# Sums of squares, inverse roots and weight preparation of a hybrid convolution and attention block, moved and rewritten

## What is computed

```python
xn = rms_norm(x, norm_mix_g)
z = xn @ w_in                      # columns B | C | h | q | k | v, 512 each
y_conv = B * (conv3(C * h) + b)    # causal, three taps per channel
q, k = rms_norm(q, q_gain), rms_norm(k, k_gain)       # over each head of 64
s = q @ k_band.T / 8 + bias        # 64-position chunks, band of 9 chunks
o = softmax(s) @ v_band
y = concat(group_rms_norm(y_conv), group_rms_norm(o)) # groups of 64
x = x + y @ w_out
xn = rms_norm(x, norm_mlp_g)
x = x + square(relu(xn @ w1)) @ w2                    # 4096 hidden
# rms_norm(v, g) = v * rsqrt(mean(v * v) + 1e-6) * g
```

## Time and profile before

| what | value |
|---|---|
| median of 3 runs | 1197.24 us (1194.58 to 1197.43) |
| the profiled execution, its own time | 1192.94 us |
| its span | 1191.0 us |
| PE busy | 1131.7 us, 95% of the span |
| weight loads of PE | 938.1 us, 79% |
| DVE busy | 762.8 us, 64% |
| POOL busy | 629.2 us, 53% |
| ACT busy | 533.7 us, 45% |
| DMA | 135.81 MB, 114 GB/s |

### The profile page before, as it was taken

How to read it: one execution, slowest core, us unless ns; L and a number is a source line. 1 busy time by engine, 2 the same in 40 slices (tenths; PEclk the granted TensorE clock), 3 DMA queues, 4 the chain that set the end, 5 groups by cost and what they waited for, 6 DMA issues and landing times.

```text
span 1191.0 us, 14699 instructions
## 1 busy us (share of the span) xinstructions
PE 1131.7 (95%) x5368; PEld 938.1 (79%) x5368; DVE 762.8 (64%) x860; ACT 533.7 (45%) x835; POOL 629.2 (53%) x349
## 2 busy tenths in 40 slices
PE   4999999999999989998799999999998999999998
PEld 4778878877887877787688888888877888888887
DVE  7567867876786787444343443435358677776788
ACT  5454454455446464313445444454544333343331
POOL 3421240322124012035668888878769699696892
PEclk9999999999999999899999999999999999999999
DMA  7210110111010142220245444444487635445324
GB/s 230 92 53 18 50 49 11 53 37 35 18 51 22 50 167 90 102 72 36 62 141 195 141 165 145 159 159 142 136 287 267 211 106 170 151 134 197 110 87 159
DMA packets 98512, 135.81 MB, mean 114 GB/s; under 512 B 8072, under 2 KB 52112, under 8 KB 98456
## 3 DMA queue, kind: packets, MB, share of 16 engines
q1 hardware_dynamic: 95104, 131.13, 32.9%
q10 hardware_dynamic: 3352, 3.94, 1.1%
HBM read 97.27 MB, written 39.34 MB: 115 GB/s over the span
## 4 chain that ended last, share of the span: by engine, by line
PE 79%; issue 8%; DVE 5%; POOL 3%; ACT 2%; DMA 1%; SPq 0%; DVEq 0%; POOLq 0%; ACTq 0%
PE PJ L1473 15%; PE SC L1727 9%; PE PJ L1727 9%; PE OS L1727 7%; PE PJ L1764 6%; PE PT L1764 6%; PE SC L1764 6%; PE OS L1764 6%; PE PJ L1549 5%; PE SC L1507 3%; PE OS L1531 2%; PE PT L1518 1%; POOL wsl L506 1%; DVE sq L1016 1%; POOL wsl L504 1%
## 5 line engine op out<-in xcount | busy, mean ns | idle before, releaser
L1473 PE MATMUL PJ<-actT,wsl 128*128 128x512 f32 (+1 forms) x1176 | 299.8, 398 | 2.4 <-POOL wsl L506 2.4
L1473 PEld LDWEIGHTS PJ<-actT,wsl 128*128 128x128 f32 x1176 | 211.8, 192 | 40.8 <-POOL wsl L506 2.8
L616 POOL TENSOR_TENSOR ring<-b,ring 128x1024 fp32r<-128x1024 f32 x48 | 137.8, 2879 | 37.8 <-ACT ring L944 37.6
L1382 DVE TENSOR_TENSOR ring<-hraw,ring 128x1024 fp32r<-128x1024 f32 x56 | 151.3, 2738 | 3.8 <-ACT ring L939 3.8
L504 POOL CAST wsl<-raw 128x1024 fp32r<-128x1024 f32 x24 | 26.9, 1121 | 199.6 <-PE PJ L1473 183.9
L939 ACT ACTIVATE ring<-hraw 128x1024 fp32r<-128x1024 f32 x56 | 59.2, 1058 | 134.4 <-PE OS L1764 62.6
L1727 PE MATMUL OS<-actT,w1a 128*128 128x512 f32 x384 | 93.4, 391 | 1.7 <-ACT p1s L880 1.7
L723 ACT ACTIVATE prob<-prob,negm 128x640 f32<-128x640 f32 (+4 forms) x64 | 44.6, 697 | 107.9 <-DVE negm L1090 107.7
L1764 PE MATMUL PJ<-ring 128*128 128x512 f32 x336 | 82.2, 395 | 6.1 <-POOL ring L616 4.5
L1016 DVE RECIPROCAL sq<-sq 128x256 f32<-128x256 f32 (+1 forms) x43 | 82.5, 1925 | 3.9 <-ACT sq L690 3.9
L1727 PEld LDWEIGHTS OS<-actT,w1a 128*128 128x128 f32 x384 | 71.6, 188 | 16.5 <-POOL w1a L557 1.9
(11 more groups left out here) (193 smaller groups left out, 2227.7 us busy)
## 6 DMA issues: line engine op xcount, KB each, us to landing
hraw<-hidd SPq DMA_DIRECT2D x56, 512.0 KB, 3.6
w1r<-in_w_mlp_in SPq DMA_DIRECT2D x16, 1024.0 KB, 6.1
hidd<-hs SPq DMA_DIRECT2D x64, 256.0 KB, 2.0
b<-in_w_mlp_out SPq DMA_DIRECT2D x16, 1024.0 KB, 6.5
raw<-in_w_in SPq DMA_DIRECT2D x24, 512.0 KB, 3.7
hidd<-h SPq DMA_DIRECT2D x48, 256.0 KB, 2.3
xin<-in_x SPq DMA_DIRECT2D x8, 512.0 KB, 8.5
woraw<-in_w_out SPq DMA_DIRECT2D x8, 512.0 KB, 7.5
```

Of the source, the lines that this page charges most:

```text
L616: nc.gpsimd.tensor_tensor(duo(n)[1][LO], W2_SRC[name][:, 2 * d:2 * d + 2], duo(n)[1][HI].bitcast(F32), ALU.subtract).then_inc(s["wl2_done" ...
L1382: vec.tensor_tensor(duo(n)[0][LO], hraw[:, n % HRING], duo(n)[0][HI].bitcast(F32), ALU.subtract).then_inc(s["hl2_done"], 1)
L1473: last = mm(PJ[:, g % 2, cols], wsl[:, w % NSLOT, a, k], actT[:, b, k, c], start=(r == 0), stop=(r == 3 * KD - 1))
```

## The change

1. **Inverse root.** `deviation` no longer takes the square root. With v the mean square plus epsilon, ACT makes r = exp(-0.5 ln v) (two activations) and w = r * r / 128 (a third, `rt`), and DVE makes one Newton step in two instructions, w = (sum + 64 eps) * w and r = (w - 1.5) * r, in place of the reciprocal. The result has the opposite sign, which cancels between q and k and is taken back in the gain of the convolution. The bank SS is now free after DVE's first instruction, not after ACT's. The norm of the attention output (`o_dev`, `o_norm`) is treated the same way. One table that holds logarithm and exponential is loaded by name before the body.
2. **Units.** The sum of squares n = 2 goes from PE's extras 1b to 2a, n = 3 from 3b to 4a; ACT's and DVE's steps behind them move by about one unit (below).
3. **Parameters.** The parameter copy and the zeroing of `ub` go from the start of DVE's iteration to 2b (`prepare`).
4. **Entry.** The order of transposes, parts and sums is another; POOL prepares the second weights only after x tile 3 is scaled, and zeroes `qz` after the third weights in place of before them.
5. **MLP.** `W1_PREP` is gone: products and preparation have one order, in which P3 and P4 of block 0 come before P6, P7, P5 of block 1. POOL's sums are made earlier. The unit transposes 8 to 12 stand at other places among the products 1 to 3, and DVE's `t13(3)` comes after `unit_lo(7)`.

```diff
-W1_ORDER = (W1_HEAD + [("P6", 1), ("P3", 0), ("P7", 1), ("P4", 0), ("P5", 1)]
+W1_ORDER = (W1_HEAD + [("P3", 0), ("P4", 0), ("P6", 1), ("P7", 1), ("P5", 1)]
...
-W1_PREP = W1_HEAD + [("P3", 0), ("P4", 0), ("P6", 1), ("P5", 1), ("P7", 1)] + W1_ORDER[12:]
...
             def deviation(it, n):
                 act.wait_ge(s["ones_done"], it * 6 + (n + 1))
-                act.activation(sq[:, zbuf(n)], SS[:, :], ACT.Sqrt, bias=eps[:, 0:1], scale=1.0 / HD).then_inc(s["ss_read"], 1)
+                act.activation(sq[:, zbuf(n)], SS[:, :], ACT.Ln, bias=eps[:, 0:1], scale=1.0 / HD).then_inc(s["dev_done"], 1)
+                act.wait_ge(s["dev_done"], it * 18 + 3 * n + 1)
+                act.activation(sq[:, zbuf(n)], sq[:, zbuf(n)], ACT.Exp, scale=-0.5).then_inc(s["dev_done"], 1)
+                act.wait_ge(s["dev_done"], it * 18 + 3 * n + 2)
+                act.activation(rt[:, n % 2], sq[:, zbuf(n)], ACT.Square, scale=(0.5 / HD) ** 0.5
+                               ).then_inc(s["dev_done"], 1)
...
             def inverse(it, n, part=None, extra=0):
+                r0, w = sq[:, zbuf(n)], rt[:, n % 2]
                 if part != 1:
+                    dve.wait_ge(s["dev_done"], it * 18 + 3 * n + 3)
+                    vec.scalar_tensor_tensor(w, SS[:, :], HD * EPS, w, ALU.add, ALU.mult).then_inc(s["ss_read"], 1)
+                if part != 0:
                     dve.wait_ge(s["ss_read"], it * 8 + (TURN[n] + 3 + extra))
-                op = vec.reciprocal(sq[:, b, c], sq[:, b, c])
+                    vec.scalar_tensor_tensor(r0, w, 1.5, r0, ALU.subtract, ALU.mult)...
...
-                    if u == 1:
+                    if u == 2:
                         deviation(it, 2)
-                    if u == 2:
                         take(it, 3)
                     if u == 3:
+                        v_copy(it, 1)
+                    if u == 4:
                         qk_hi(it, 2)
-                        v_copy(it, 1)
                         deviation(it, 3)
-                    if u == 4:
+                    if u == 5:
                         v_hi(it, 1)
-                    if u == 5:
+                        c_copy(it, 0)
                         qk_hi(it, 3)
...
             for r in range(3 * KD):
+                if r in (2, 12):
+                    x_transpose(6 + r // 8)
+                if r == 6:
+                    sum_squares(0, 0, 1)
+                if r == 20:
+                    sum_squares(0, 1, 1)
                 group_product(0, 2, r)
-                if r == 14:
-                    sum_squares(0, 1, 1)
```

More of the change, by code:

```diff
@@ L499, in weights @@
                     sl = w % NSLOT
+                    if w == 1 and first:
+                        pool.wait_ge(s["xs_done"], 4)
                     pool.wait_ge(raw_in[w % 2], it * (NW // 2 * 16) + 16 * (w // 2 + 1))
@@ L507, in weights @@
                                             ALU.subtract).then_inc(s["w_ready"], 1)
+                    if w == 2 and first:
+                        pool.wait_ge(s["tr_done"], NT)
+                        pool.wait_ge(s["w_ready"], 3)
+                        for slot in QZ:
+                            nc.gpsimd.memset(qz[HEADS[0], :, slot, :].bitcast(F32), 0.0).then_inc(s["qz_zero"], 1)
+                        pool.wait_ge(s["qz_zero"], len(QZ))
                     if w == 2:
                         pool.wait_ge(s["sqh_done"], it * 6 + 2)
+                        pool.wait_ge(s["rsc_done"], it * 2 + 1)
                         nc.gpsimd.tensor_tensor(sql[:, 1], sq[:, 1], sqh[:, 1].bitcast(F32), ALU.subtract
@@ L522, in weights @@
                         pool.wait_ge(s["qlo_done"], it * 2 + 2)
-                    if w == 1 and first:
-                        pool.wait_ge(s["tr_done"], NT)
-                        pool.wait_ge(s["w_ready"], 2)
-                        for slot in QZ:
-                            nc.gpsimd.memset(qz[HEADS[0], :, slot, :].bitcast(F32), 0.0).then_inc(s["qz_zero"], 1)
-                        pool.wait_ge(s["qz_zero"], len(QZ))
             weights(0, True)
@@ L732, in o_dev @@
                 act.wait_ge(s["oss_done"], it * 2 + (g + 1))
[L733 removed]
+                act.activation(osd[:, :], oss[:, :], ACT.Ln, bias=eps[:, 0:1], scale=1.0 / HD).then_inc(s["osd_done"], 1)
+                act.wait_ge(s["osd_done"], it * 4 + (2 * g + 1))
+                act.activation(osd[:, :], osd[:, :], ACT.Exp, scale=-0.5).then_inc(s["osd_done"], 1)
             def o_store(it, g):
@@ L838, in _ @@
             take(0, 0)
-            x_hi(NT - 2)
-            x_hi(NT - 1)
+            x_hi(4)
+            x_hi(5)
+            take(0, 1)
+            x_hi(6)
             deviation(0, 0)
-            take(0, 1)
+            x_hi(7)
             deviation(0, 1)
@@ L998, in _, with x_lo @@
             dve.wait_ge(s["g_in"], 16)
-            for t in range(NT):
+            def x_lo(t):
+                dve.wait_ge(s["xhi_done"], t + 1)
+                lo_part(t, slice(t * P, (t + 1) * P))
+            for t in range(3):
                 x_scale(t)
-                if t >= 2:
-                    dve.wait_ge(s["xhi_done"], t - 1)
-                    lo_part(t - 2, slice((t - 2) * P, (t - 1) * P))
+            x_lo(0)
+            x_scale(3)
+            for t in range(1, 4):
+                x_lo(t)
+            for t in range(4, NT):
+                x_scale(t)
             def squares_lo(it, n):
@@ L1213, in extras, with prepare @@
                     inverse(it, 5, 1)
-            def iteration(it, last):
+            def prepare(it):
                 dve.wait_ge(s["ss_read"], it * 8 + 4)
@@ L1219, in iteration @@
                 vec.memset(ub[:, 0:2], 0.0).then_inc(s["halo_done"], 1)
+            def iteration(it, last):
                 dve.wait_ge(s["bias_in"], it * 64 + 64)
@@ L1259, in _ @@
             squares_lo(0, 0)
-            for t in (NT - 2, NT - 1):
-                dve.wait_ge(s["xhi_done"], t + 1)
-                lo_part(t, slice(t * P, (t + 1) * P))
+            for t in range(4, NT):
+                x_lo(t)
             dve.wait_ge(s["prm_in"], 16 * 10)
@@ L1410, in _ @@
                     hid_sums(W1_ORDER[g - 2][1])
-                if g >= 11 and W1_ORDER[g - 1][0] == "P4":
+                if g == 11:
+                    hid_sum4(0)
+                if g > 11 and W1_ORDER[g - 1][0] == "P4":
                     hid_sum4(W1_ORDER[g - 1][1])
@@ L1767, in duo_products @@
                 return last
-            for n, u in ((1, 7), (2, 9), (3, 11)):
-                unit_transpose(u)
-                product(n, range(6))
-                unit_transpose(u + 1)
-                product(n, range(6, 12))
+            unit_transpose(7)
+            product(1)
+            unit_transpose(8)
+            product(2, range(4))
+            unit_transpose(9)
+            product(2, range(4, 8))
+            unit_transpose(10)
+            product(2, range(8, 12))
+            product(3, range(4))
+            unit_transpose(11)
+            product(3, range(4, 8))
+            unit_transpose(12)
+            product(3, range(8, 12))
             for j in range(3):
```

109 lines of the change are left out of this document (57 added, 52 removed).

## The result

| | before | after |
|---|---|---|
| median of 4 runs | 1197.34 us (1194.58 to 1197.67) | 1165.65 us (1165.04 to 1165.69) |
| the profiled execution, its own time | 1192.94 us | 1165.66 us |
| its span | 1191.0 us | 1163.6 us |
| PE busy | 1131.7 us | 1121.9 us |
| DVE busy | 762.8 us | 715.9 us |

The ratio is 0.974, 95% interval 0.972 to 0.976: 31.7 us less, where I had forecast 24 less (1173).

A forecast was written before the change was run, and what follows sets the result against it. PE was taken as the bound (79% of the chain), with its idle time and half-clock time to win. Terms A to F sum to -24.0 us, 1192.9 to 1168.9; plus the 4.3 offset, 1173, range 1162 to 1188.

The forecast's parts named there:

- A: Entry: earlier fourth transpose and no wait for third weights, against new waits for SS and v; -1.3 us.
- B: Loop body: waits for low squares and product with v go, two smaller waits per iteration come; -2.3 us.
- C: PE clock in the body: one of two clock losses behind the 2.1 us waits goes; -1.7 us.
- D: Iteration starts and unit 13 of the last: parameter-copy wait goes, half of a 2.1 wait counted; -3.8 us.
- E: Second norm: gain-load wait and clock loss go, later ACT part of w_out costs 1.3; -4.6 us.
- F: Head of the MLP: 13.4 us lost there shrink to 3.1 through the new product order; -10.3 us.
- The offset: Whole kernel: profiled execution stands 4.3 us below the median, added to 1168.9 to forecast the median.
- Hidden steps: Rival, body: the two new waits don't show as DVE catches up, and the clock holds; 1164 us, chance 0.17.
- Blocked Newton steps: Rival, body: POOL's subtraction holds the second Newton step, 2 us low-squares wait and clock losses return; 1183 us, chance 0.19.
- Units as the bound: Rival, body: longer ACT chain and bunched DVE steps lengthen all 64 units; 1211 us at 0.6 each, chance 0.03.
- Nothing moves: Rival: POOL bounds the MLP head, its wait moves to P3, body gives back its gain; within 0.3%, chance 0.05.

The follow-up runs named there:

- old_entry: Changed kernel with the entry's order of the kernel before put back, exponential form kept: 1169.3 us, ratio 0.977.
- all_waits: Changed kernel plus reordered steps in entry, body, last iteration, w_out and second MLP product, low squares of block 3 ahead of Newton steps: 1151.42 us, ratio 0.963.
- copy_at_start: Changed kernel with the tiny parameter copy put back at the start of the iteration: 1173.1 us, ratio 0.980.
- both_undone: Changed kernel with square root and reciprocal, and the old units for blocks 2 and 3, put back; entry, copy and MLP order stay new: 1177.79 us, ratio 0.985.
- sqrt_in_new_places: Changed kernel with ACT's square root and DVE's reciprocal put back, new places, entry and MLP order kept: 1182.85 us, ratio 0.990.
- before_again: The kernel before, unchanged, profiled once more to see whether its clock losses recur at the same places: 1194.37 us.
- mlp_only: Kernel before with only the head of the MLP in its new order: 1185.4 us, ratio 0.992.

## Why the prediction was right, and by how much not

The direction, the places and the new waits were right, and 1165.65 lies in the range; the gain was 31.7 instead of 24. By profile against profile it is 27.4 us of span against 24.0.

The waits were priced by the idle time in brackets. Measured from the start of one matmul to the start of the next, less the shortest such step between the same two kinds of matmul in these traces, a wait in the body costs 0.15 to 0.25 us more than its bracket. For the scores of unit 8 this is to be seen above: 1.10 less 0.03 is 1.07, the bracket has 0.83. "Start to start" below means this. By term:

- **A, entry, -1.3 forecast, -3.0 measured** (`old_entry`: 2.7 to 3.7). The fourth transpose starts 1.85 earlier (21.04 to 19.19; 1.7 forecast), the 2.4 went, the new wait for SS is 2.30 (1.9 forecast) and that for v 0.46 (0.9): -1.9 - 2.4 + 2.3 + 0.5 = -1.5. The term had no place for what follows the fourth transpose. There PE's matmuls of 256 columns come 0.21 apart at first and 0.12 later. In the kernel before the slow steps last until 26.8, in the changed kernel until 21.3, and that is the missing 1.4. First the kernel before, 12 matmuls in 2.91 us, then the changed one, 49 in 6.43:

```profile
22.63 2.91 PE L1473 MATMUL PJ<-actT,wsl 128*128 128x256 f32 x12
...
20.78 6.43 PE L1513 MATMUL PJ<-actT,wsl 128*128 128x256 f32 x49
```

  The slow steps fall in a stretch (20 to 30) whose granted clock reads 1.00 in both profiles; what makes them slow, no run here shows. PE stood still for 2.47 ahead of the fourth transpose before, and for 0.58 in the changed kernel.
- **B, body, -2.3 forecast, about -4.8 measured.** The new waits have 0.29, 0.83 and 0.21 (at unit 4) in brackets, but start to start they cost 0.46, 1.08 and 0.37, in four iterations 7.5, and 7.6 was forecast. `all_waits` agrees: there the three are gone, and its looped iterations are 1.9 shorter each. The sum of 1.9 is in part luck, since it was made of 0.6, 1.3 and 0: the blocked Newton step, priced at nothing, cost 0.37 after all, and the others less. ACT's six activations, three of `deviation` and three of `take`, run back to back in 3.47 us (3.56 by my addition), and begin 0.1 sooner ahead of PE's need than `take` alone had. Of the 0.7 of lateness that I passed on to unit 7, 0.46 was there: `pt_lo` ends at 184.83, 0.34 behind the place where the scores would have started (184.49); before, it ended 0.12 ahead of them. What the term had wrong is what goes away, read off the brackets: start to start the four waits for low squares were 8.9 and not 8.2, those of the product with v 2.7 and not 1.7, and some small steps give 0.7 more.
- **C, clock in the body, -1.7 forecast.** Both losses went, not one of two: 3.4 by the windows, 3.1 by the slower steps of the matmuls in them. Since which of the waits costs a clock loss changes between executions, the loss of the kernel before is not two windows but a number that varies; the changed kernel has no wait over 0.83 in its looped iterations and showed no loss there in either of its two profiles.
- **D, starts and last iteration, -3.8 forecast.** At the starts the 2.7 went (3.2 start to start), in the last iteration 0.4 instead of 1.1 (2.1 to 1.72: the convolution step there took 2.71 beside POOL). So -3.6. `copy_at_start` shows that the move is worth 6.5 to 7.4 in the new kernel, as the copy there meets POOL at two starts instead of one.
- B, C and D together: -7.8 forecast, -12.3 by the table. -4.8 - 3.1 - 3.6 = -11.5, and the rest is spread over steps of PE that are each under 0.12 us longer than the shortest.
- **E, second norm, -4.6 forecast, -3.5 measured** (w_out 36.96 to 35.43; first to eighth transpose 70.61 to 68.66). The gain's load no longer holds PE (2.77 to 0.38), and the later part of w_out costs 1.55 where PE had waited 0.4 before, close to the 1.3 priced. With the square root put back, the wait ahead of the first transpose is back too (2.8 in `both_undone`, 3.3 in `sqrt_in_new_places`). The clock term was too large: 3.1 taken, 1.95 gained. The first profile was a bad one (0.66); before_again has 0.83 there and needs only 0.6 more than the changed kernel for that stretch.
- **F, head of the MLP, -10.3 forecast, -9.8 measured.** The new waits are where they were said to be, but are 0.27, 0.77 and 0.78, together 1.8 where I left 3.1; on the other hand the work that I took as 36.7 is 38.5 (40.27 less 1.8). These two errors nearly cancel. Behind these waits PE runs through to the third P1, and the same 9.8 come with this part alone. Here the row behind the earlier trace rows in the new order:

```profile
544.50 1.16 PE L1764 MATMUL OS<-actT,w1a 128*128 128x512 f32 x4 [0.78 <-ACT p1s L900]
...
573.80 2.43 PE L1764 MATMUL OS<-actT,w1a 128*128 128x512 f32 x10
```

- The rest of the stretch, first product and second, is +1.2.
- **The offset, 4.3 us.** I carried the distance of the profiled execution from the median of before (1192.94 to 1197.24) over to the changed kernel. Its profiled execution stands on its median (1165.66, 1165.65). The offset was part of a spread of 6.6 us that goes with the clock: of the 32 executions the ten with a mean granted clock of 0.989 or more took 1192.5 to 1195.7, the other 22 (0.985 to 0.988) 1193.6 to 1199.1, and the profiled one had 0.991. Those of the changed kernel have 0.996 to 0.999. So the offset belonged into the sum as a gain. The two profiles of before add a second part, whether the parameter copy meets POOL (a wait of 2.2 or 0.3). This and term B are the steps that failed most.

**The rivals.** Hidden steps (1164) came nearest in time, but by luck: it took the 7.6 of the new waits and one clock loss as gone, and the new waits cost 7.5. The time came from the offset, the entry and the waits removed. Blocked Newton steps (1183): the block is there, at 0.37 each instead of 2.1. Units as the bound (1211): the iterations are 2.2 to 5.1 us shorter. It shows up in part where the square root stays in the new places: lateness passed from unit to unit, 5 us in all. Nothing moves: refuted by `mlp_only`.

## What to carry to other kernels

Price a shorter operation and its new place together: here the form alone gave 6 us, the places alone cost 5, and both together gave 11 to 12. When a wait is moved, look first at what runs on the neighbour engine at that moment: a DVE subtraction, Newton step or even tiny copy from SBUF to SBUF that starts under a POOL subtraction ends only after it, so it belongs ahead of it or behind it. Count a wait from the start of the matmul ahead of it to the start of the one behind it, on both sides of the sum: the brackets left out 1.7 us of the two groups of waits that went. And read more than one execution before taking over an offset between a profile and a median: it may be just what the change removes.
